# Residual sum in the tile of x, hn one turn later, and transposes in fours: an encoder layer on one core

## What is computed

```python
def rmsnorm(x, g):
    y = x * lax.rsqrt(jnp.mean(x * x, axis=-1, keepdims=True) + 1e-6)
    return y * g

hn = rmsnorm(x, ln_mix_pre)
x  = x + rmsnorm(stick_breaking_mixer(hn, w_qkv, w_o), ln_mix_post)
hn = rmsnorm(x, ln_ffn_pre)                       # <- the change is about here
x  = x + rmsnorm(swiglu_ffn(hn, w_gu, w_down), ln_ffn_post)

def swiglu_ffn(h, w_gu, w_down):
    g, u = jnp.split(h @ w_gu, 2, axis=-1)
    return (jax.nn.silu(g) * u) @ w_down
```

## Time and profile before

| | us |
|---|---|
| median of three runs | 1299.03 |
| profiled execution, time | 1298.36 |
| profiled execution, span | 1296.3 |
| TensorE busy in the span | 1240.9 |
| VectorE busy | 943.6 |
| ScalarE busy | 648.6 |
| GpSimd busy | 501.0 |

### The profile page before, as it was taken

One profiled execution on the slowest core, in us unless ns is written; L12 is line 12 of the kernel. 1 busy time (PEld: TensorE's weight loads), 2 busy tenths in 40 slices (PEclk: granted clock), 3 DMA queues, 4 the chain that ended last, 5 costly groups with the idle time before them and its releaser, 6 DMA issues.

```text
span 1296.3 us, 17929 instructions
## 1 busy us (share of the span) xinstructions
PE 1240.9 (96%) x6288; PEld 1046.5 (81%) x6288; DVE 943.6 (73%) x1088; ACT 648.6 (50%) x1205; POOL 501.0 (39%) x394
## 2 busy tenths in 40 slices
PE   6999999999999996997789999999999999999997
PEld 6888888888888885886568888888888888888886
DVE  7689989998989889524666656676665677584557
ACT  5677777676767777433342333232233243464443
POOL 2111110110101100043327766666676667584443
PEclk9999999999999999998899999999999999999999
DMA  5010110000101001433224444444444447985643
GB/s 214 30 33 17 33 33 18 33 16 32 33 16 33 16 17 63 133 79 84 81 82 164 145 163 172 138 162 179 155 154 163 154 155 273 333 292 190 197 136 130
DMA packets 65915, 147.50 MB, mean 114 GB/s; under 512 B 5168, under 2 KB 13360, under 8 KB 65840
## 3 DMA queue, kind: packets, MB, share of 16 engines
q1 hardware_dynamic: 64400, 141.32, 31.8%
q10 hardware_dynamic: 1440, 5.24, 1.5%
HBM read 106.43 MB, written 40.11 MB: 113 GB/s over the span
## 4 chain that ended last, share of the span: by engine, by line
PE 85%; DVE 7%; DMA 4%; POOL 2%; ACT 1%; issue 1%; DVEq 0%; SPq 0%; POOLq 0%; ACTq 0%
PE bank L1805 11%; PE bank L1809 11%; PE bank L1807 11%; PE bank L1627 6%; PE bank L1628 6%; PE bank L1629 6%; PE bank L1885 5%; PE bank L1886 5%; PE bank L1887 5%; PE bank L1727 4%; PE bank L1701 3%; DMA x2d<-acc 3%; PE bank L1703 3%; PE bank L1747 2%; PE bank L1746 2%; POOL acc L1126 1%
## 5 line engine op out<-in xcount | busy, mean ns | idle before, releaser
L1075 POOL TENSOR_TENSOR w_lo<-raw,w_hi 128x1024 fp32r<-128x1024 f32 x21 | 51.8, 2468 | 368.6 <-ACT w_hi L731 368.6
L1287 DVE TENSOR_TENSOR_SCAN stay<-stay,diag_one 128x256 f32<-128x256 f32 (+7 forms) x128 | 180.2, 1408 | 3.7 <-ACT stay L847 3.7
L1477 DVE TENSOR_TENSOR wl<-wraw,wh 128x512 fp32r<-128x512 f32 x77 | 105.4, 1394 | 72.1 <-ACT wh L1004 72.1
L739 ACT ACTIVATE AT_hi<-bank 128x512 fp32r<-128x512 f32 (+1 forms) x160 | 89.1, 557 | 135.2 <-PE bank L1727 134.4
L1115 POOL TENSOR_TENSOR wl<-tl,wh 128x512 fp32r<-128x512 f32 x66 | 97.7, 1482 | 136.8 <-DVE t2f L1401 105.3
L1166 POOL TENSOR_TENSOR hl<-raw,hh 128x512 fp32r<-128x512 f32 x77 | 112.1, 1469 | 78.1 <-ACT hh L1002 77.6
L1805 PE MATMUL bank<-S_hi,wh 128*128 128x512 f32 x348 | 136.3, 392 | 2.7 <-POOL wl L1115 2.7
L1809 PE MATMUL bank<-S_hi,wl 128*128 128x512 f32 x348 | 135.9, 390 | 0.0
L1807 PE MATMUL bank<-S_lo,wh 128*128 128x512 f32 x348 | 135.9, 390 | 0.0
L1627 PE MATMUL bank<-hnT_hi,w_hi 128*128 128x512 f32 x336 | 134.2, 399 | 0.0
L1628 PE MATMUL bank<-hnT_lo,w_hi 128*128 128x512 f32 x336 | 132.2, 393 | 0.0
(11 more groups left out here) (171 smaller groups left out, 3036.0 us busy)
## 6 DMA issues: line engine op xcount, KB each, us to landing
raw<-in_units SPq DMA_DIRECT2D x76, 512.0 KB, 4.2
raw<-hops SPq DMA_DIRECT2D x77, 256.0 KB, 3.6
wdr<-in_units SPq DMA_DIRECT2D x22, 512.0 KB, 6.3
wsums<-wdT SPq DMA_DIRECT2D x11, 1024.0 KB, 4.9
hops<-S SPq DMA_DIRECT2D x11, 1024.0 KB, 4.9
wraw<-wsums SPq DMA_DIRECT2D x44, 256.0 KB, 3.4
hops<-H SPq DMA_DIRECT2D x11, 768.0 KB, 3.3
wraw<-in_units SPq DMA_DIRECT2D x33, 256.0 KB, 3.8
```

The source lines that it names most:

```text
L1287: nc.vector.tensor_tensor_scan(st, st, diag_one[:, 0:w], 0.0, ALU.mult, ALU.add).then_inc(scan_done, 1)
```

## The change

Five things are changed.
1. The addition of x writes its result into the tile of x (`x_in`) and leaves the scaled tile in `acc` as it is. The store to `x2d`, the square and `hn` read `x_in`. `hn(t)` writes to `acc` and no longer waits for the store. `hn7` and `s1_last` are gone.
2. On VectorE `hn(t - 1)` stands in turn t, after `mix_scale(t)` and the low parts. `pair_sums(p)` stand one turn later too.
3. The loads into `x_in` go from ScalarE's queue to SP's. The load for tile t+2 waits for `hn(t)`, for the square and for the landed store of tile t. Set 1's load goes out in turn 5, in the middle of this, and not after the eight stores. `load_down(0)` waits for the last stores instead of the end of the transposes; GpSimd's `weight_sums(0)` takes over that wait. The tiles `raw23`, `wdr` and `wraw` lie elsewhere.
4. Set 0's four sums of weights are made in turn 4, in place of the blocks in `raw`. Their low parts on GpSimd stay after turn 7. Set 1's T2 comes before the join of H21, its T1 before that of H22.
5. The 20 units after turn 7 go in five groups of four: S2, S3, A22, S1 of each pair, and all S4 last. TensorE's order is group 0, P1, Q1, group 1, P2, Q2, groups 2 and 3, P6, group 4, P7, P4, P5. S4 is first used in set 1. A unit waits for the one sum that it reads, no longer for all four.

In the diff `...` marks what is left out.

```diff
-NORM_UNITS += [(k, p) for p in range(4) for k in ("S2", "S3", "A22", "S1", "S4")]
+NORM_UNITS += [(k, p) for p in range(4) for k in ("S2", "S3", "A22", "S1")]
+NORM_UNITS += [("S4", p) for p in range(4)]
+SUM_ORDER = ["S1", "S3", "S2", "S4"]
...
-PRODUCTS0 = [("P1", 0, "A11"), ("P2", 1, "A12"), ("Q1", 2, "A11"), ("Q2", 3, "A12"),
+PRODUCTS0 = [("P1", 0, "A11"), ("Q1", 2, "A11"), ("P2", 1, "A12"), ("Q2", 3, "A12"),
...
+        def sum_place(s, name, k):
+            if s == 0:
+                return set_blocks(0)[{"T3": "B22", "T1": "B12", "T2": "B11", "T4": "B21"}[name]]
+            return t2f[:, :] if name == "T2" else tl(k)
...
-            for t in range(NT):
-                sp.wait_ge(x2_ready, t + 1)
-                sp.dma_start(x2d[t].rearrange("p (k c) -> p k c", c=P), x2(t)).then_inc(x2_out[t], 16)
...
-            load_set(1)
+            for t in range(NT):
+                sp.wait_ge(x2_ready, t + 1)
+                sp.dma_start(x2d[t], x_in[:, t % 2, :]).then_inc(x2_out[t], 16)
+                if t + 2 < NT:
+                    sp.wait_ge(hn_ready, NT + t + 1)
+                    sp.wait_ge(sq_done, square_index("x2", t) + 1)
+                    sp.wait_ge(x2_out[t], 16)
+                    sp.dma_start(x_in[:, t % 2, :], x_tiles[:, TILE[t + 2], :]).then_inc(x_again[t % 2], 16)
+                if t == 5:
+                    sp.wait_ge(mix_full, 12)
+                    load_set(1)
             sp.wait_ge(hn_ready, 2 * NT)
-            sp.wait_ge(t_full, T_END)
+            for t in (NT - 2, NT - 1):
+                sp.wait_ge(x2_out[t], 16)
             load_down(0)
...
             def x2_square(t):
                 act.wait_ge(x2_ready, t + 1)
-                if t + 2 < NT:
-                    act.dma_start(x_in[:, t % 2, :], x_tiles[:, TILE[t + 2], :]).then_inc(x_again[t % 2], 16)
                 act.wait_ge(sq_done, square_index("x2", t))
-                nc.scalar.activation(blocks(junk_t[:, :]), x2(t), ACT.Square,
+                nc.scalar.activation(junk_t[:, :], x_in[:, t % 2, :], ACT.Square,
...
-            pair_hi(0)
+            four_hi(0)
             copy_p1(0)
+            sum_hi(0, "T2", 0)
             x2_square(NT - 1)
-            pair_hi(1)
-            act.wait_ge(prod_full, prod_count(0, "P1"))
-            sum_hi(0, "T2", 0)
+            four_hi(1)
+            act.wait_ge(prod_full, prod_count(0, "P2"))
             sum_hi(0, "T3", 1)
-            pair_hi(2)
             sum_hi(0, "T1", 2)
+            four_hi(2)
+            act.wait_ge(prod_full, prod_count(0, "Q2"))
             sum_hi(0, "T4", 3)
-            pair_hi(3)
+            four_hi(3)
+            four_hi(4)
...
-                nc.gpsimd.tensor_tensor(x2(t), x2(t), blocks(x_in[:, t % 2, :]), ALU.add).then_inc(x2_ready, 1)
+                nc.gpsimd.tensor_tensor(blocks(x_in[:, t % 2, :]), x2(t), blocks(x_in[:, t % 2, :]),
+                                        ALU.add).then_inc(x2_ready, 1)
...
             def hn(t):
                 dve.wait_ge(rstd_done, NT + 2 * t + 2)
-                if t < NT - 1:
-                    dve.wait_ge(x2_out[t], 16)
-                nc.vector.scalar_tensor_tensor(out=hn7[:, :, :] if t == NT - 1 else x2(t), in0=x2(t),
+                nc.vector.scalar_tensor_tensor(out=x2(t), in0=blocks(x_in[:, t % 2, :]),
...
-                if t < 6:
-                    hn(t)
-                if t in (4, 5):
-                    pair_sums(t - 4)
+                if t >= 1:
+                    hn(t - 1)
+                if t == 4:
+                    for name, k in (("T3", 1), ("T1", 2), ("T2", 0), ("T4", 3)):
+                        weight_sum(0, name, k)
+                if t in (5, 6):
+                    pair_sums(t - 5)
             hn(6)
-            pair_low(0, 0, 3)
+            pair_sums(2)
             mix_scale(NT - 1)
-            pair_low(0, 3, 5)
-            pair_sums(2)
-            pair_low(1)
-            weight_sum(0, "T3", 1)
-            weight_sum(0, "T2", 0)
-            pair_low(2)
+            four_low(0)
             hn(7)
             pair_sums(3)
-            weight_sum(0, "T1", 2)
-            weight_sum(0, "T4", 3)
-            pair_low(3)
+            for n in range(1, 5):
+                four_low(n)
...
-            dve.wait_ge(prod_full, prod_count(0, "P4"))
-            dve.wait_ge(comb, comb_count(0, "q"))
-            joined(H21, bank[3][:, :], u2[:, :])
             for e in range(2):
                 dve.wait_ge(f_in[2 + e], 16)
             weight_sum(1, "T3", 3)
+            weight_sum(1, "T2", 1)
+            dve.wait_ge(comb, comb_count(0, "q"))
+            joined(H21, bank[3][:, :], u2[:, :])
             dve.wait_ge(prod_full, prod_count(0, "P5"))
+            weight_sum(1, "T1", 2)
             joined(H22, bank[2][:, :], p1[:, :])
-            weight_sum(1, "T1", 2)
-            weight_sum(1, "T2", 1)
...
-            pair_transpose(0)
+            four_transposes(0)
             pe.wait_ge(mix_scaled, 2 * (NT - 1))
             pe.wait_ge(t_lo, norm_unit(NT))
-            pe.wait_ge(f_lo, w_count(0, "B11"))
+            pe.wait_ge(f_lo, w_count(0, "B22"))
             product(bank[0], 0, "A11", True)
-            pair_transpose(1)
+            product(bank[1], 2, "A11", True)
+            four_transposes(1)
             pe.wait_ge(p1_done, 1)
-            pe.wait_ge(f_lo, w_count(0, "B21"))
             product(bank[0], 1, "A12", False)
-            pair_transpose(2)
-            pe.wait_ge(f_lo, w_count(0, "B12"))
-            product(bank[1], 2, "A11", True)
-            pe.wait_ge(f_lo, w_count(0, "B22"))
             product(bank[1], 3, "A12", False)
-            pair_transpose(3)
+            four_transposes(2)
+            four_transposes(3)
             pe.wait_ge(mix_scaled, 2 * NT)
-            pe.wait_ge(t_lo, norm_unit(NT + 15) + 1)
+            pe.wait_ge(t_lo, norm_unit(NT + 12) + 1)
             pe.wait_ge(f_lo, w_count(0, "T2"))
             product(bank[2], 0, "S2", True)
+            four_transposes(4)
...
```

More of the change, by code:

```diff
@@ L276, in w_count @@
     return PREP0.index(slot) + 1 if s == 0 else len(PREP0) + 7 * (s - 1) + PREP.index(slot) + 1
-T_ORDER0, T_ORDER = ["T3", "T2", "T1", "T4"], ["T3", "T1", "T2", "T4"]
+T_ORDER1, T_ORDER = ["T3", "T2", "T1", "T4"], ["T3", "T1", "T2", "T4"]
 def t_count(s, name):
-    return 4 * s + (T_ORDER if s else T_ORDER0).index(name) + 1
+    return 4 * s + (T_ORDER1 if s == 1 else T_ORDER).index(name) + 1
 COMB0 = ["m11", "m12", "q", "c21", "c22", "m21", "m22"]
@@ L452, in hn_half @@
         def hn_half(t, c):
-            return hn7[:, 4 * c:4 * c + 4, :] if t == NT - 1 else x2(t, c)
+            return x2(t, c)
         def s1_of(p):
-            return s1_last[:, :, :] if p == 3 else s1_t[:, p, :, :]
+            return s1_t[:, p % 3, :, :]
         def norm_source(u):
@@ L907, in norm_hi, with four_hi @@
                     t_hi_copy(n, norm_dest(u, 0), norm_bank(n)[:, :].rearrange("p (k c) -> p k c", k=4))
-            def pair_hi(p):
-                norm_hi(range(NT + 5 * p, NT + 5 * p + 5))
+            def four_hi(n):
+                norm_hi(range(NT + 4 * n, NT + 4 * n + 4))
             def first_split(name):
@@ L943, in sum_hi @@
                 act.wait_ge(t_add, t_count(s, name))
-                nc.scalar.activation(wh(k), t2f[:, :] if name == "T2" else tl(k), ACT.Copy).then_inc(f_hi, 1)
+                nc.scalar.activation(wh(k), sum_place(s, name, k), ACT.Copy).then_inc(f_hi, 1)
             def block_hi(s, name, k):
@@ L1112, in sum_lo @@
                 pool.wait_ge(f_hi, w_count(s, k if s else name))
-                if name == "T3":
+                if s and name == "T3":
                     pool.wait_ge(t_add, t_count(s, "T2"))
-                nc.gpsimd.tensor_tensor(wl(k), t2f[:, :] if name == "T2" else tl(k), wh(k).bitcast(F32),
+                nc.gpsimd.tensor_tensor(wl(k), sum_place(s, name, k), wh(k).bitcast(F32),
                                         ALU.subtract).then_inc(f_lo, 1)
@@ L1143, in weight_sums @@
                     pool.wait_ge(wsum_out, 16 * g)
+                else:
+                    pool.wait_ge(t_full, T_END)
                 b11, b12, b21, b22 = (wdr[:, e, c * HALF:(c + 1) * HALF] for e in range(2) for c in range(2))
@@ L1362, in norm_low, with four_low @@
                              norm_dest(u, 0))
-            def pair_low(p, a=0, e=5):
-                norm_low(range(NT + 5 * p + a, NT + 5 * p + e))
+            def four_low(n):
+                norm_low(range(NT + 4 * n, NT + 4 * n + 4))
             def pair_sums(p):
@@ L1390, in weight_sum @@
                     dve.wait_ge(t_add, t_count(s, "T3"))
[L1391 to L1393 removed]
+                    if s > 1:
+                        dve.wait_ge(f_lo, w_count(s - 1, 1))
+                    i0, i1, alu = sum_place(s, "T3", 3), b["B11"], ALU.add
                 else:
                     dve.wait_ge(t_add, t_count(s, "T2"))
[L1396 to L1401 removed]
```

(17 more changed lines are left out.)

30 lines of the change are left out of this document (9 added, 21 removed).

## The result

The kernel after takes 1277.03 us (median of four runs, 1275.74 to 1279.53) against 1298.41 for the kernel before in the same series: a ratio of 0.9836, 95% interval 0.9818 to 0.9854. It is 21.4 us faster; 27 were forecast. The time lies in the forecast range, but just above 1276, where the likeliest case ended.

What follows compares the result with a forecast made beforehand. TensorE bounds the kernel; only its idle and slow time can be won. Stage 68.7 + 1.2 + 0.9 + 0.4 + 1.8 = 73.0 against 98.8, plus 1.6 slow clock: 27.4 us less, 1271.6; range 1267.5 to 1282.

Steps and rivals of the forecast that it cites:

- the likeliest case: Whole kernel: the change works as forecast, 1267.5 to 1276 us, chance 0.73.
- rival A: Turns stay slow: VectorE/GpSimd lock holds more often or x_in loads come late; 9 to 10 us not won, 1281; chance 0.13.
- rival B: End stage: GpSimd's roots and low parts hold hn(7) and sums 3 us more, clock drops 2.3; 1277; chance 0.08.
- What bounds the kernel, and that a gain is passed on: TensorE works 96% of the span; a change ahead of 700 us is passed on to the end one for one.
- The store is off the turn: VectorE no longer waits for the store, 5.9 us; a turn becomes 8.5 or 9.4 us, below TensorE's 11.8.
- hn against the addition: VectorE against GpSimd: the addition waits 1.3 us in turns 1 and 2; from turn 3 hn waits 1.1.
- The walk through the turns: Turns 1 to 3, addition to mix_scale: of 7.75 us idle before the second pair of transposes, 1.2 is left.
- the sign of A: TensorE idle over 3 us before the transposes of turns 4 to 6.
- Item 2, the chain behind the last projection: VectorE's 13.8 us chain just covered by TensorE's 14.2; then VectorE paces the next eight units: 0.9 us.
- The low-clock stretches are gone: TensorE, 540 to 700 us: the stretches at the lower clock, 6.5 us lost in all before, should vanish.
- SP's queue and the early sums: Late x_in load covered by 3 us in turn 4; four sums, 2.8 us, fit VectorE's room there; cost nil.
- Items 3 and 4: First S2 product waits 0.4 us for its last low part; set 1's second product waits 1.8, then full clock.

Runs made afterwards that it cites:

- same_turn: The kernel after with hn(t) in turn t instead of t+1, still without a wait for the store: 1276.73 us, ratio 0.9833 to the kernel before.
- turn_part: The kernel before with changes 1 to 3 alone (sum in x_in, later hn, loads on SP), end of the stage as before: 1286.28 us.
- load_after: The kernel before with only the load of x_in(t+2) moved, issued by SP once the store of tile t has landed: 1289.36 us.

## Why the prediction was right, and where it was not

The time, 1277.03, is 5.4 us above the 1271.6 of the sum. It lies in the range, but just beyond 1276, in the part that was added for rivals A and B.

- *What bounds the kernel, and that a gain is passed on.* Right: from 700 on TensorE stays busy and the rest of the span is the same to 0.1 us, once the slow stretch is counted.
- *The store is off the turn.* Right as to VectorE's wait. What the prediction took as given was the store's 5.9 us; they were made by the load beside it. A version that only parts the two wins 9.2 us, so a good part of the gain credited to the wait has a cheaper source. The later hn, which the change joined to it, was not needed (same_turn).
- *hn against the addition.* Right in size: 1.0 for 1.3 in turns 1 and 2, 1.1 from turn 3. The rule of the Trainium skill that stood there (SBUF — State Buffer, SBUF: two separate sides) holds for hn too, as these rows show.
- *The walk through the turns.* This term was mis-sized. It took 4.7 and 5.6 us from the addition to the mix norm's root out of rows in which o_lo ran at another time; it was 5.6 and 6.6. With the store's wait gone o_lo starts as soon as its high part is there, and that is when GpSimd makes the root. The prediction's sum had this only as "a microsecond more" in turn 3, and halved. Its rival A named the mechanism (o_lo, GpSimd's small instructions, the splits), but at 2 to 3 us a turn and with a chance of 0.13; it was 0.7 to 1.1 us a turn. Additions end at 556.34, 566.81, 578.35 and 588.88, turns of 10.5, 11.5 and 10.5 instead of 9.8, 10.7 and 9.4. The first pause was 3.05 instead of 1.2, just over the 3 us that the prediction gave as the sign of A.
- *Item 2, the chain behind the last projection.* Mis-sized too: T3's and T1's low parts were not counted against the sums (2.1 us), nor the sums of pair 2 against the mix norm's root (L1133 and L1093 took 0.55 and 0.64 instead of 0.2 each). Pause and eight units took 7.9 us where 3.2 + 0.9 were forecast. This is rival B in its mechanism, with 2.3 us of pause for its 3, on top of the forecast's first pause.
- *The clock.* "The low-clock stretches are gone" was wrong for two of three: 1.7 us behind each pause.
- *SP's queue and the early sums.* Right: none of GpSimd's eight additions waited for a load, and the four sums (2.61 us in turn 4) opened no pause.
- *Items 3 and 4.* No pause for item 3. The last pause was 1.61 us for 1.8, with the full clock behind it.

In sum: 1.85 too little for the first pause, 1.7 for the clock behind it, 3.8 for groups 2 and 3 with their clock, less 0.6 for items 3 and 4: 6.75 of the 6.98 us by which the stage, 79.98 us when counted from the last issue as the prediction did, was longer than 73.0. One sum of the prediction is off by a little: with no pause left, 1271.6 less 4.3 is 1267.3 and not 1267.5.

## What to carry to other kernels

When a wait is taken out of a loop, list which instructions now meet on VectorE and GpSimd, the tiny ones too: a sum of 128 numbers on the path, held by a neighbour's 1.2 us, cost 0.9 to 1.0 us in each of three turns, nearly as much as the neighbour. Ask of a slow transfer what was issued beside it before building an order that hides it. And test the parts of a bundle in both directions: here one half alone won 12.3, the other 4.2, and the one delay that looked central, hn's, won nothing.

## What the runs showed of the hardware

- A store of 512 KB landed in 5.9 us with a load of 512 KB issued beside it, and in 3.2 alone, in pieces of 512 bytes out of `acc`; out of `x_in` it took 2.6 in rows of 4 KB and 2.9 in pieces (medians). With a load issued 0.4 us ahead of it, rows of 4 KB took 4.5 to 5.3 (the kernel after).
- Instructions of GpSimd on 128x1 elements took 1.11 to 1.19 instead of 0.20 us beside a VectorE subtract of two SBUF tiles. A pair of subtracts with one input in a bank took its 1.28 us beside the addition, before and after (the pair of turn 3, 586.36 to 587.64).
- Pauses of TensorE of 3.05 and 2.28 us were followed by a granted clock of 0.68 and 0.65 for about 5 us, one of 1.61 was not. In the kernel before a pause of 2.30 was not followed by it either. The length alone doesn't decide: behind the pause of 2.67 before set 1's second product the clock was 0.51 in the kernel before and 1.00 in turn_part (672.6 to 676.0), and a pause of 2.00 in turn_part was followed by 0.50 (654.1 to 656.0), one of 2.01 in load_after by 1.00 (655.4 to 660.0). What else decides is open.
